# A hybrid decoder step on one core: the token row of the expert products in SBUF or in PSUM

## The chip, the cores and the metric

The kernel runs on one core of one Trainium2 chip. The metric is the time of one execution on the device in microseconds, the median of several runs. The engines of the core are TensorE (PE in the profile; its weight loads are PEld), VectorE (DVE), ScalarE (ACT), GpSimd (POOL) and SyncE (SP). They share 16 DMA engines.

## What is computed

One layer of a decoder trunk, for 512 prompt tokens and 8 sample tokens, all in float32, D_MODEL = 1024. The first part (normalisation, an S5 and a Mamba-2 branch, an output projection) is not touched here. The second part is a retrieval of experts: every token asks 8 heads, every head finds 16 out of 16384 experts by two top-16 lists and a top-16 of their 256 sums, and every expert is one row of `expert_down` and one row of `expert_up`:

```
qv = (xb @ w_query).reshape(128, 8, 2, 128)
s = einsum('thsd,hskd->thsk', qv, keys)
sv, si = top_k(s, 16)                       # two halves of the key
fv, fi = top_k(sums of all pairs, 16)       # 16 experts of 16384
g = softmax(fv)
u = expert_down[eidx]                       # (token, head, 16, 1024)
act = gelu(einsum('thkd,td->thk', u, xb)) * g
v = expert_up[eidx]
out = einsum('thk,thkd->td', act, v)
```

For 520 tokens these are 520 x 128 rows of 4 KB from each of the two tables, 545 MB in all.

## The kernel before

The program runs in stages, one after the other. The last, `stage_peer`, holds the retrieval. Tokens lie in 4 blocks of 128 (one token to a partition), the samples in a last short block in which 64 partitions hold 8 tokens x 8 heads.

A **unit** is one head of one block: 32 units of tokens. A **step** g is half a unit, 8 of its 16 experts (`GATE = 8`); there are 64 steps of tokens and two of samples (`NSTEP` = 66, steps 64 and 65). The engines each have their own order of work, written out by hand, and meet in semaphores:

- GpSimd issues for every step 8 **down gathers** (`gather_down`, L1659): each is one indirect DMA that brings one expert's row of 1024 floats to each of the 128 tokens, 512 KB, into one buffer of a ring. Then it issues 8 **up gathers** (`gather_up`, L1675) of the step that lies `LAG = 4` steps back. The down gathers of an even step wait for the unit's top-k (`s_top`), and every second gather waits until the buffers it fills were read (`s_uused`, counted in products). Up gathers wait until TensorE has used the rows of the group before (`s_vused`).
- VectorE runs, for every step, 8 **products** (`products`, L1903): one instruction multiplies a gathered buffer by the token row and sums it up to one number per token; the product is written back over the buffer. The token row is `hb`, 128 x 1024, the block's normalised input, copied from `h2` once per block (L1943 and L1947). The sample steps take `x64`, which lies in SBUF, in its place. Between the products of an even and an odd step stands the top-k of the next unit (`topk`, L1859 to L1894). In units 0 to 6 VectorE also stores scores from PSUM. In the third unit of blocks 1 to 3 it closes the block before (L1921, L1923, L1934, L1938), in unit 8 it takes in the sample rows and in unit 9 the scales of the last normalisation.
- ScalarE makes gelu and softmax, and spreads the weights into the matrix Z.
- TensorE projects the queries and scores them in units 0 to 6, and sums the up rows with their weights (`add`, L1797 for tokens, L1805 for samples).

**Buffers.** SBUF is one tensor, `arena`, laid out by hand. Sixteen buffers of 128 x 1024 floats (`rows16`) lie where earlier stages had their data: the first 8 are those of the up rows, the other 8 belong to the ring of the down rows. Two more, `more`, lie behind the query's memory, and two, `late`, in the memory of the query weights, free only after unit 7. The ring is therefore `first_U` = 8 + 2 = 10 buffers in steps 0 to 15 (gathers 0 to 127) and `all_U` = 12 from step 16 (gather 128) on. What a gather waits for follows from the list of what was last in its buffer (`U_free`):

```
first_U, all_U = rows16[VR:] + more, rows16[VR:] + more + late
for i in range(GATE * NSTEP):
    ring = first_U if i < 2 * PH * GATE else all_U
    s = i % len(first_U) if i < 2 * PH * GATE else (i - 2 * PH * GATE) % len(all_U)
    U_free.append(used.get(s))
...
if j % 2 == 0 and U_free[i + 1] is not None:
    pool.wait_ge(s_uused, U_free[i + 1] + 1)
```

With rings of 10 and 12 an even gather i waits until i - 8 and i - 10 products are done; gather 128 is the first of the larger ring, which begins again at buffer 0: it waits until product 121 is done.

`hb` lies in PSUM before the change, banks 6 and 7.

Of the kernel before, what the change touches and what calls it, by code (L numbers as in the profile page):

```python
# [28 lines left out]
D = 1024  # L29
# [1497 lines left out]
def stage_peer(nc, mem, sem, ps, A, O, mod_d, integers):  # L1527
# [8 lines left out]
    def take(*shape, rows=P):  # L1536
        nonlocal M
        M += int(np.prod(shape))
        return mem(M - int(np.prod(shape)), *shape, rows=rows)
# [6 lines left out]
    late = [take(D) for _ in range(2)]  # L1546
    assert M <= Map.PEER
    M = Map.PEER
    more = [take(D) for _ in range(2)]
    Z = take(4, 8, 32)  # L1550
    sel64 = take(PH, NS, rows=NS)
    r64 = take(NS)
# [14 lines left out]
    sdiag = take(2 * GATE, NS)  # L1567
    stat, rstd = take(1), take(1)
    assert M <= Map.W, M
    hb = ps[:, 6:8, :].rearrange("p a n -> p (a n)")  # L1570
    idx = [integers["expert0"], integers["expert1"]]
    idxT = [integers["rows0"], integers["rows1"]]
    kix, fix, fiju, iotai = (integers[n] for n in ("keys", "pairs", "halves", "counting"))
# [426 lines left out]
def program(nc, A, O):  # L2000
    with nc.cleanup_on_exit(), ExitStack() as ctx:
        mem = Arena(ctx.enter_context(nc.sbuf_tensor("arena", [P, Map.W], F32)))
        ps = ctx.enter_context(nc.psum_tensor("ps", [P, 8, 512], F32))
        mod_d = nc.dram_tensor("mod_scratch", (NC_ROWS, NMOD * D), F32, kind="Internal").ap()
        bc_d = nc.dram_tensor("bc_scratch", (NS, D), F32, kind="Internal").ap()

        integers = {name: ctx.enter_context(nc.sbuf_tensor(name, [P, n], dtype))[:, :] for name, n, dtype in
                    (("expert0", TOPK, U32), ("expert1", TOPK, U32), ("keys", 2 * TOPK, U32), ("pairs", TOPK, U32),
                     ("halves", 2 * TOPK, U32), ("counting", TOPK, I32), ("rows0", 2 * TOPK, U32), ("rows1", 2 * TOPK, U32))}


        s_s5, s_ssd = nc.alloc_semaphore("first_s5"), nc.alloc_semaphore("first_ssd")

        for stage, more in ((constants, ()), (stage_condition, (ps, A, mod_d, s_s5)),
                            (stage_s5, (ps, A, O, s_s5, s_ssd)), (stage_ssd, (ps, A, O, bc_d, s_ssd)), (stage_query, (ps, A, mod_d)),
                            (stage_peer, (ps, A, O, mod_d, integers))):
            with nc.cleanup_on_exit():  # L2017
                stage(nc, mem, nc.alloc_semaphore, *more)
# [29 lines left out]
```

## Time and profile before

| | us |
|---|---|
| median of 3 runs (lowest, highest) | 2483.84 (2475.89, 2489.05) |
| the profiled execution, its own time | 2482.62 |
| its span (first to last instruction) | 2480.7 |
| VectorE busy | 1510.9 (61%) |
| GpSimd busy | 1090.3 (44%) |
| TensorE matmuls busy | 1365.7 (55%) |
| moved by GpSimd's DMA queue | 545.33 MB |

A busy time is a sum over the whole span, in which the expert stage is only the last 1500 us; what an engine is worth there has to be read from slices, groups and the timeline. A gather of 128 rows counts as busy on GpSimd while its descriptors are made, not while its data moves. A product is written CUSTOM_DVE_ANT_0 in the profile, and its tiles say where its inputs are: `arena` is SBUF, `ps` is PSUM.

### The profile page before, as it was taken

To read this page: it belongs to the slowest core of one execution; us is meant where nothing else is said; L and a number is where in the kernel's file an instruction comes from. 1 tells how busy PE (TensorE), PEld (TensorE's weight loads), DVE (VectorE), ACT (ScalarE), POOL (GpSimd) and SP (SyncE) were. 2 spreads that over 40 slices of the span, in tenths; PEclk is the share of its full clock that TensorE was granted. 3 is DMA by queue.
4 is the path that set the end of the run, shared out by engine and by line. 5 is a ranking of instruction groups with operands and counts; after the bars stand their busy time and mean duration, and the time that the engine had idled before them with its cause. 6 is when DMAs were issued, how large, how long until landed. Compare 5 with 4: busy or idle time off the path is not lost.

```text
span 2480.7 us, 19709 instructions
## 1 busy us (share of the span) xinstructions
PE 1365.7 (55%) x6380; PEld 764.8 (31%) x6380; DVE 1510.9 (61%) x3235; ACT 279.0 (11%) x575; POOL 1090.3 (44%) x1154
## 2 busy tenths in 40 slices
PE   4697997999644998556652222233233233233265
PEld 0276674878633845443320000000000000000010
DVE  0454998165688123777667776767776767676411
ACT  1011000111112002111110110000110001010000
POOL 0122000010130000476767777777777777777632
PEclk7798998999766999787866666655656665665555
DMA  9821000221332050799999999999999999999854
GB/s 367 315 64 52 34 34 0 87 73 37 94 94 93 2 189 26 296 365 403 409 403 409 409 406 409 409 406 405 406 401 396 409 409 405 408 403 407 279 145 152
DMA packets 209033, 651.98 MB, mean 263 GB/s; under 512 B 26192, under 2 KB 52464, under 8 KB 204793
## 3 DMA queue, kind: packets, MB, share of 16 engines
q0 software_dynamic: 150016, 545.33, 56.6%
q1 hardware_dynamic: 58092, 103.70, 11.8%
q10 hardware_dynamic: 824, 1.70, 0.2%
q8 instruction: 51, 0.84, 0.1%
q14 instruction: 50, 0.41, 0.0%
HBM read 643.24 MB, written 7.54 MB: 262 GB/s over the span
## 4 chain that ended last, share of the span: by engine, by line
DMA 21%; POOL 15%; issue 10%; PE 7%; DVE 7%; DVEq 0%; POOLq 0%; ACT 0%
DMA arena<-in_expert_up_dram,rows 16%; POOL arena L1675 8%; POOL arena L1659 7%; DMA arena<-in_expert_down_dram,expert 5%; PE ps L1797 4%; DVE arena L1903 2%; PE ps L1805 2%; DVE arena L1862 0%; DVE arena L1861 0%; PE ps L1344 0%; DVEq L1855 0%; DVE keys L1860 0%; DVE arena L1888 0%; DVE arena L1885 0%; DVE arena L1889 0%
## 5 line engine op out<-in xcount | busy, mean ns | idle before, releaser
L1797 PE MATMUL ps<-arena 128*32 128x512 f32 x2048 | 409.8, 942 | 831.1 <-DMA arena<-in_expert_up_dram,rows 831.1
L1903 DVE CUSTOM_DVE_ANT_0 arena<-arena,ps 128x1024 f32<-128x1024 f32 x512 | 617.1, 1219 | 317.0 <-DMA arena<-in_expert_down_dram,expert 301.7
L1675 POOL DMA_INDIRECT arena<-in_expert_up_dram,rows x512 | 490.6, 958 | 241.0 <-issue 136.4
L1659 POOL DMA_INDIRECT arena<-in_expert_down_dram,expert x528 | 501.3, 949 | 200.8 <-issue 155.8
L1797 PEld LDWEIGHTS ps<-arena 128*32 128x32 f32 x2048 | 81.9, 146 | 1120.1 <-issue 1120.0
L546 PE MATMUL ps<-arena 128*128 128x260 f32 x896 | 207.7, 391 | 14.8 <-ACT arena L477 7.8
L546 PEld LDWEIGHTS ps<-arena 128*128 128x128 f32 x896 | 173.0, 194 | 52.3 <-issue 16.2
L954 POOL MEMSET arena<- 128x528 f32 x2 | 1.1, 538 | 305.2 <-POOLq L2017 305.2
L1344 PE MATMUL ps<-arena 128*128 128x260 f32 x512 | 124.4, 404 | 4.9 <-POOL counting L1642 3.4
L1071 PE MATMUL ps<-arena 128*128 128x260 f32 x512 | 112.5, 383 | 0.0
L1344 PEld LDWEIGHTS ps<-arena 128*128 128x128 f32 x512 | 102.0, 202 | 28.9 <-issue 6.3
L1071 PEld LDWEIGHTS ps<-arena 128*128 128x128 f32 x512 | 97.2, 190 | 14.9
L1700 ACT ACTIVATE arena<-arena 128x8 f32<-128x8 f32 (+1 forms) x66 | 13.7, 208 | 748.1 <-DVE arena L1903 748.1
L970 POOL TENSOR_TENSOR arena<-arena 128x1024 f32<-128x1024 f32 x8 | 19.8, 2483 | 165.5 <-DVE arena L1230 126.7
L1459 PE MATMUL ps<-arena 128*128 128x512 f32 (+1 forms) x160 | 71.5, 610 | 8.2 <-DMA arena<-in_w_out_dram 8.2
L269 PE MATMUL ps<-arena 128*32 128x512 f32 x256 | 49.2, 910 | 44.8 <-DMA arena<-in_w_ada_dram 35.5
L1921 DVE TENSOR_TENSOR arena<-ps,arena 128x1024 f32<-128x1024 f32 (+1 forms) x5 | 6.1, 1220 | 91.6 <-PE ps L1805 70.7
L1805 PE MATMUL ps<-arena 64*8 64x512 f32 x64 | 54.8, 1053 | 5.7 <-DMA arena<-in_expert_up_dram,expert 5.7
L1167 PE MATMUL ps<-arena 128*128 128x260 f32 x256 | 57.5, 388 | 0.0
L456 POOL MEMSET arena<- 128x4096 f32 x1 | 3.5, 3512 | 113.4 <-POOLq L2017 113.4
L469 POOL COPY arena<-arena 64x16 f32<-64x16 f32 x64 | 31.6, 547 | 49.1 <-DVE arena L720 49.1
L1167 PEld LDWEIGHTS ps<-arena 128*128 128x128 f32 x256 | 49.5, 194 | 7.8
(347 smaller groups left out, 1878.4 us busy)
## 6 DMA issues: line engine op xcount, KB each, us to landing
arena<-in_w_ada_dram SPq DMA_DIRECT2D x12, 2048.0 KB
arena<-in_w_in_dram SPq DMA_DIRECT2D x11, 2048.0 KB, 8.4
arena<-in_expert_down_dram,expert POOLq DMA_INDIRECT x528, 12.6
arena<-in_w_ada_final_dram SPq DMA_DIRECT2D x4, 2048.0 KB
arena<-in_w_query_dram SPq DMA_DIRECT2D x8, 1024.0 KB, 16.4
arena<-in_expert_up_dram,rows POOLq DMA_INDIRECT x512, 12.1
out_dram<-arena SPq DMA_DIRECT2D x13, 512.0 KB, 2.9
arena<-in_x_prompt_dram SPq DMA_DIRECT2D x2, 2048.0 KB
```

The costliest lines, as they stand in the source:

```text
L269: last = nc.tensor.matmul(ps[strip(j, 32), i, :], cT[:, k, :], ring[q][:, k % 2, 512 * j:512 * j + 512], start=(k == 0), stop=(k == KD - 1))
L469: last = nc.gpsimd.tensor_copy(flat[:, 160 * q + 16 * g:160 * q + 16 * g + 16], bb[rows, j, 4 * ut + q, :])
L546: last = nc.tensor.matmul(ps[:, 5 + h, 0:HALF], ring[i % 2][:, k, m * P:(m + 1) * P], hT[:, k, h * HALF:(h + 1) * HALF], start=(k == 0), s ...
L1071: last = mm(ps[:, 2 * (n % 2) + h, 0:HALF], ring[i % 2][:, k, m * P:(m + 1) * P], hT[:, k, h * HALF:(h + 1) * HALF], start=(k == 0), stop= ...
L1167: last = mm(ps[:, 4 + 2 * (m % 2) + h, 0:HALF], brw[:, k, m * P:(m + 1) * P], cv[:, k, h * HALF:(h + 1) * HALF], start=(k == 0), stop=(k = ...
L1344: last = nc.tensor.matmul(ps[:, 2 + h, 0:HALF], self.ring[(t // 2) % 2][:, k, (t % 2) * P:(t % 2 + 1) * P], self.h2T[:, k, h * HALF:(h + 1 ...
L1459: last = mm(ps[0:n, 2 * (b % 2) + j, :], mg[:, k, b * P:b * P + n], wo[:, k, j * 512:(j + 1) * 512], start=(k == 0), stop=(k == KD - 1))
L1659: G.indirect_dma_start(U[i][0:rows, :], None, down, bass.IndirectOffsetOnAxis(ap=idx[u % 2][0:rows, k:k + 1], axis=0))\
L1675: G.indirect_dma_start(Vr[j], None, up, bass.IndirectOffsetOnAxis(ap=at, axis=0))\
L1797: last = mm(ps[32 * j:32 * j + 32, c, :], Z[:, j, m, :], Vr[4 * half + j][:, c * 512:(c + 1) * 512], start=(p % 4 == 0 and m == 0), stop=( ...
L1805: last = mm(ps[0:NS, 2 + c, :], sdiag[0:64, k, :], Vr[4 * half + j][0:64, c * 512:(c + 1) * 512], start=(k == 0), stop=(k == 2 * GATE - 1))
L1903: V.tensor_tensor_reduce(U[i][0:rows, :], U[i][0:rows, :], row, 1.0, 0.0, ALU.mult, ALU.add, dots[g % 2][0:rows, j:j + 1]).then_inc(s_uuse ...
```

## The change

`more` gets one buffer in the place of two, and the memory of the other becomes `hb`; the line that put `hb` into PSUM goes. Everything else follows from that: the rings have 9 and 11 buffers, an even gather waits until i - 7 and i - 9 products are done, gather 128 waits until product 127 is done (gather 127 was the last in buffer 1), the copies at L1943 and L1947 write to SBUF, and the 512 token products at L1903 read both inputs from SBUF. Banks 6 and 7 of PSUM stay empty in this stage.

```diff
--- before.py
+++ after.py
@@ -1546,7 +1546,8 @@
     late = [take(D) for _ in range(2)]
     assert M <= Map.PEER
     M = Map.PEER
-    more = [take(D) for _ in range(2)]
+    more = [take(D)]
+    hb = take(D)
     Z = take(4, 8, 32)
     sel64 = take(PH, NS, rows=NS)
     r64 = take(NS)
@@ -1567,7 +1568,6 @@
     sdiag = take(2 * GATE, NS)
     stat, rstd = take(1), take(1)
     assert M <= Map.W, M
-    hb = ps[:, 6:8, :].rearrange("p a n -> p (a n)")
     idx = [integers["expert0"], integers["expert1"]]
     idxT = [integers["rows0"], integers["rows1"]]
     kix, fix, fiju, iotai = (integers[n] for n in ("keys", "pairs", "halves", "counting"))
```

## Rows read from the trace of the kernel before

**Rows 1.** Page, part 2: GB/s in 40 slices of the span, 62 us each.
```profile
GB/s 367 315 64 52 34 34 0 87 73 37 94 94 93 2 189 26 296 365 403 409 403 409 409 406 409 409 406 405 406 401 396 409 409 405 408 403 407 279 145 152
```

**Rows 2.** Page, part 5: line, tiles xcount | busy, mean ns | idle.
```profile
L1903 DVE CUSTOM_DVE_ANT_0 arena<-arena,ps 128x1024 f32<-128x1024 f32 x512 | 617.1, 1219 | 317.0 <-DMA arena<-in_expert_down_dram,expert 301.7
L1675 POOL DMA_INDIRECT arena<-in_expert_up_dram,rows x512 | 490.6, 958 | 241.0 <-issue 136.4
L1659 POOL DMA_INDIRECT arena<-in_expert_down_dram,expert x528 | 501.3, 949 | 200.8 <-issue 155.8
```

**Rows 3.** Timeline, steps 16, 24, 25, 63: start, length (us), what.
```profile
1315.66 0.93 POOL L1659 DMA_INDIRECT arena<-in_expert_down_dram,expert  x1 [0.31 <-issue]
...
1316.90 0.94 POOL L1659 DMA_INDIRECT arena<-in_expert_down_dram,expert  x1 [0.30 <-issue]
...
1503.00 1.22 DVE L1903 CUSTOM_DVE_ANT_0 arena<-arena,ps 128x1024 f32<-128x1024 f32 x1
...
1504.28 1.22 DVE L1903 CUSTOM_DVE_ANT_0 arena<-arena,ps 128x1024 f32<-128x1024 f32 x1
...
1508.42 0.93 POOL L1659 DMA_INDIRECT arena<-in_expert_down_dram,expert  x1 [0.30 <-issue]
...
1515.85 1.21 DVE L1903 CUSTOM_DVE_ANT_0 arena<-arena,ps 128x1024 f32<-128x1024 f32 x1
...
2294.24 0.94 POOL L1659 DMA_INDIRECT arena<-in_expert_down_dram,expert  x1 [0.31 <-issue]
```

**Rows 4.** Waits of GpSimd, 1000 to 2300 us: total us, times, longest.
```profile
POOL arena L1675 <- PE ps L1797: 53.9, 46, 5.5
```

**Rows 5.** Groups by shape, VectorE, 900 to 2480 us: sample products.
```profile
L1903 DVE CUSTOM_DVE_ANT_0 arena<-arena 64x1024 f32<-64x1024 f32 x16 | 19.1, 1215 | 31.8 <-DMA arena<-in_expert_down_dram,expert 31.5
```

**Rows 6.** Timeline, GpSimd and VectorE, sample products (step 64).
```profile
2342.12 1.21 DVE L1903 CUSTOM_DVE_ANT_0 arena<-arena 64x1024 f32<-64x1024 f32 x1
...
2342.16 1.98 POOL L1675 DMA_INDIRECT arena<-in_expert_up_dram,rows  x1 [0.30 <-issue]
...
2343.26 1.21 DVE L1903 CUSTOM_DVE_ANT_0 arena<-arena 64x1024 f32<-64x1024 f32 x1
...
2344.41 1.21 DVE L1903 CUSTOM_DVE_ANT_0 arena<-arena 64x1024 f32<-64x1024 f32 x1
...
2344.45 1.99 POOL L1675 DMA_INDIRECT arena<-in_expert_up_dram,rows  x1 [0.30 <-issue]
...
2345.56 1.21 DVE L1903 CUSTOM_DVE_ANT_0 arena<-arena 64x1024 f32<-64x1024 f32 x1
...
2346.74 0.94 POOL L1675 DMA_INDIRECT arena<-in_expert_up_dram,rows  x1 [0.30 <-issue]
```

**Rows 7.** Timeline at the closing of the first block of tokens.
```profile
1442.95 1.28 DVE L1934 SCALAR_TENSOR_TENSOR arena<-arena 128x1024 f32<-128x1024 f32 x1
...
1443.43 1.61 POOL L1659 DMA_INDIRECT arena<-in_expert_down_dram,expert  x1 [0.30 <-issue]
```

**Rows 8.** Timeline, the first two of the eight products of step 21.
```profile
1433.82 1.21 DVE L1903 CUSTOM_DVE_ANT_0 arena<-arena,ps 128x1024 f32<-128x1024 f32 x1
...
1434.96 1.22 DVE L1903 CUSTOM_DVE_ANT_0 arena<-arena,ps 128x1024 f32<-128x1024 f32 x1
```

**Rows 9.** Timeline: gathers of steps 2, 4, 15; last product of 15.
```profile
1023.17 0.94 POOL L1659 DMA_INDIRECT arena<-in_expert_down_dram,expert  x1 [14.95 <-DVE expert L1894]
...
1031.88 0.94 POOL L1659 DMA_INDIRECT arena<-in_expert_down_dram,expert  x1 [0.30 <-issue]
...
1056.89 0.94 POOL L1659 DMA_INDIRECT arena<-in_expert_down_dram,expert  x1 [14.13 <-DVE expert L1894]
...
1295.46 0.94 POOL L1659 DMA_INDIRECT arena<-in_expert_down_dram,expert  x1 [0.30 <-issue]
...
1316.15 1.22 DVE L1903 CUSTOM_DVE_ANT_0 arena<-arena,ps 128x1024 f32<-128x1024 f32 x1
```

**Rows 10.** Page, part 6: DMA issues, count, median us to landing.
```profile
arena<-in_expert_down_dram,expert POOLq DMA_INDIRECT x528, 12.6
```

## What the change does to the time, forecast before it was run

> **What bounds the kernel now.** I read the slices of the span first [rows 1]: from about 1080 us to 2310 us the 16 DMA engines are full and move some 405 to 409 GB/s. That is the expert stage, and the change touches nothing else. The groups by cost [rows 2] name its parts: 512 products on VectorE (L1903) with 317 us of idle time before them, so VectorE is not the limit; and 528 down and 512 up gathers on GpSimd, which issues them one by one. Next I looked for the second limit behind the DMA engines. In the timeline one gather follows the other after 1.24 us (1315.66 to 1316.90), so a step of 16 gathers needs 16 x 1.24 = 19.8 us of GpSimd; the products come every 1.28 us (1503.00 to 1504.28), one transfer of the full DMA engines, so a step needs 16 x 1.28 = 20.5 us of DMA; and from step 16 (1315.66) to step 63 (2294.24) a step really takes 978.6 / 47 = 20.82 us [rows 3]. GpSimd thus has about 1.0 us of slack in a step, 5%. It shows in the waits as 53.9 us in which GpSimd waited for the up products on PE (L1797), 46 times [rows 4]. The kernel is bound by DMA with GpSimd right behind.
>
> **The change part by part.** *The product itself.* Its second input moves from PSUM to SBUF. The same operation with both inputs in SBUF is in the trace: the 16 sample products, 1215 ns against 1219 ns [rows 2, 5]. Between -4 and +4 ns on 512 products is at most 2 us of an engine that idles 317 us: nothing.
>
> *What two SBUF inputs do to a gather.* This term decides. The sample products run back to back at 2342.12, 2343.26, 2344.41 and 2345.56, each 1.21 us. The gather issued at 2342.16 takes 1.98 us instead of 0.94, the next (2344.45) 1.99, and the one at 2346.74, which starts as the last product ends, again 0.94 [rows 6]. At the end of a block of tokens, a gather issued at 1443.43 beside a two-input operation that runs from 1442.95 to 1444.23 takes 1.61 [rows 7]. All three fit one reading: about 0.13 us after its start a gather reads its indices from SBUF; if a VectorE operation with two SBUF inputs runs then, it waits until that one ends, and has 0.81 us left: 2343.33 + 0.81 = 2344.14, as in the row; 1444.23 + 0.81 = 1445.04, as in the row. Beside token products, whose row stands in PSUM, nothing of the kind happens: over all 512 up gathers the mean is 958 ns [rows 2]. After the change all 512 token products do what the sample products do.
>
> The Trainium skill (SBUF — State Buffer, section Who interferes with whom) says the same in general: a VectorE instruction with two SBUF inputs contends with a GpSimd instruction that reads SBUF, and whichever issues first holds the shared pair for its whole length. The rows agree with the first half and not with the second: the product at 2343.26 starts and ends in 1.21 us while the gather of 2342.16 still runs. By the rule's second half VectorE would also lose time; that is the fourth rival.
>
> *What that costs in a step of the long stretch.* The eight products fill about 10.2 us of 20.8. A gather that meets them at a random point waits on average half a product, 0.61 us. After that the two engines march together: released at the end of a product, GpSimd tries again 0.81 + 0.30 + 0.13 = 1.24 us later, and if products come every 1.28 us [rows 3] the next one ends 0.04 us after that. So the other seven cost 0.04 each, 0.3 us. If the down gathers, themselves delayed, come in with a gap, the meeting at a random point happens a second time; I take one and a half meetings, 0.9 us. Where a product follows after less than 1.24 us (data already there: 1.14, as at 1433.82 [rows 8]), the gather just misses the end and waits for the one after: period 2.28, 1.04 us lost per gather, as in the sample rows. I take a third of a miss per step, 0.4 us. Need of GpSimd: 19.8 + 0.9 + 0.3 + 0.4 = 21.4, against 20.8 now: +0.6 us. Lower bound of the step's extra: 0, if all of it fits into the slack. Upper: all products at 1.14, four gathers at 2.28 in 9.1 us, +4.2 and the meeting 0.6, less the slack of 1.0: +3.8. I take the value near the rows of 1.28, since a longer step makes products wait for arrivals, which spaces them at 1.28 again. 43 ordinary steps x 0.6 = +26 us; +0 to +163.
>
> *Five steps with a late VectorE* (three closings of a block, and the two that take in the sample rows and the final scales) run their products at 1.14 [rows 8]: 4.2 + 0.6 - 1.0 = +3.8 each, +19 us; between 0 and +24.
>
> *Steps 4 to 15*, with the query projection beside them, take (1295.46 - 1056.89) / 11 = 21.7 us [rows 9], slack 1.9. Odd steps have more products at 1.14 behind the score stores: a pair loses about 1 + 4.2 = 5.2 against a slack of 3.8; six pairs, +8 us; 0 to +25.
>
> *Steps 0 to 3* are bound by the chain product, top-k, gather. The eight gathers from 1023.17 to 1031.88 run beside products at 1.14; at 2.28 they take 16 us instead of 8.7, some 7 us more, of which about 5 reach the last product and the top-k that frees the gather at 1056.89 [rows 9]. Two such pairs: +10 us; 0 to +15. Nothing later gives this back, since the DMA engines are full from there on.
>
> *The rings.* With 10 buffers the first gather of a step waits for all products of the step before the last, with 9 for one product more; with 12 and 11 the gather at place 4 of a step needs two and three products of the step before. The gather at 1508.42 is one at place 4; all eight of those products had ended by 1504.28 + 1.22 = 1505.50 [rows 3]. So one buffer costs nothing there, and would not even if a step ran 2.9 us late. At the change of rings (gather 128) there is one place: it now needs product 127, which starts at 1316.15, while the gather was issued at 1315.66 [rows 3, 9]: 1316.15 + 1.22 - 1315.66, 1.7 us, once. Taken: +2 us; 0 to +6 with the first steps.
>
> *Four copies of the token row* pass over 1024 elements as a product does, 1219 ns [rows 2]. No row here stands for one within SBUF; each can save at most those 1.2 us, or cost half as much again. The first lies in the wait for the first gather, the others in VectorE's idle time: 0 (-4 to +2).
>
> Sum: 26 + 19 + 8 + 10 + 2 = +65 us. The profiled execution took 2482.62 us (span 2480.7), 1.2 below the median 2483.84, so the sum gives 2548 by the one and 2549 by the other. I say **2548 us**, +2.6%.
>
> **The rivals.** (1) *Absorbed.* The waits of the long stretch fit the slack of 1.0 us (0.6 + 0.3 = 0.9), VectorE's late steps too; what is left is steps 0 to 3 and the ring: +0 to +12, 2490 us. For it: the waits for PE [rows 4]. Against: it leaves 0.1 us, so any miss breaks it. (2) *The slow cadence wins.* Products stay bunched at 1.14, gathers at 2.28: 43 x 3.8 + 24 + 25 + 15 = +227, 2710 us. Counting from the other side gives the same size: half of 1040 gathers meet a product and wait 0.6 each, 310 us, less 60 steps' slack of 1.0, +250. Against: the ordinary steps run at 1.28. (3) *Not slower.* A step takes 20.82 where 16 transfers need 20.5; if this 0.3 is the price of about ten gathers queued at the DMA engines (12.6 us from issue to landing, 1.28 each [rows 3, 10]), a GpSimd that issues a little later gives it back in 47 steps, -15 us, provided its need stays below 20.5, that is, waits of at most 0.7 a step, and the first steps lose nothing: 2468 us. Against: one and a half meetings alone are 0.9. (4) *Held both ways.* A gather also stops products: each of the two waits for the other, 1.22 + 0.94 = 2.16 us a product, two steps of VectorE 16 x 2.16 + 10.3 of top-k (1505.50 to 1515.85 [rows 3]) = 44.9 against 41.6 now; 3.3 / 2 x 60 = +99, 2582 us. Against: the product at 2343.26. (5) *Only the rings matter* and the token products don't disturb gathers (the row moves but nothing waits): +2 to +15 with 12 ring-bound steps of one transfer each, 2490 us. Against it: [rows 6]. The same section of the Trainium skill infers that a two-tensor operation leaves the making of descriptors alone, since it takes only the read side of the pair; by that this rival would win, but the 1.98 us of a gather beside such an operation speak against it.
>
> **How the numbers follow.** My forecast (waits with the 1.28 cadence, with its own spread 2515 to 2600) 0.58; between it and the slow cadence, ending at 2600 to 2710, 0.19; held both ways 0.05; absorbed 0.11; rings alone 0.03; not slower 0.04. The range 2500 to 2665 leaves out the absorbed cases, the gain and the top of the slow cadence, about 2 in 10. A measurement here tells about 0.5% (12 us) from no change: slower 0.85, within 0.12, faster 0.03; half of the absorbed case and most of the "not slower" case fall within.
>
> **What would show it.** Right: down and up gathers beside token products with durations from 0.95 to 2.0 us, mean duration of L1675 and L1659 up from 0.95 to about 1.02 to 1.1 (each 0.1 us is 104 us of GpSimd, of which the slack takes some 55); the ordinary step about 21.4 us; GpSimd's wait for PE L1797 almost gone; DMA slices between 390 and 400 GB/s; gather to landing shorter than 12.6 us, since fewer are queued; products still 1.22 us. Wrong: gathers at 0.94 beside products (then 5), products longer than 1.22 (then 4), most spacings 1.14 with gathers at 1.98 (then 2), waits of gathers for L1903 growing (the rings).

## The result, and the profile after

The changed kernel took 2498.13 us (median of 5 runs, 2494.81 to 2504.29), the kernel before 2480.41 on the same chip: ratio 1.0072, interval 1.0045 to 1.0099, 18 us slower. A second set gave 1.0077 (1.0061 to 1.0093). The direction was forecast; 65 us were forecast and 18 came, below the range.

The page of the changed kernel (span, part 1, part 2, groups, landing), to be read against [rows 1, 2, 10]:

```profile
span 2496.2 us, 19710 instructions
...
GB/s 367 312 77 38 34 34 0 87 73 36 93 93 94 31 158 66 254 359 403 409 406 386 387 392 409 409 408 409 399 409 409 408 407 391 395 409 407 314 126 151
...
L1903 DVE CUSTOM_DVE_ANT_0 arena<-arena 128x1024 f32<-128x1024 f32 (+1 forms) x528 | 640.6, 1225 | 367.4 <-DMA arena<-in_expert_down_dram,expert 351.3
L1675 POOL DMA_INDIRECT arena<-in_expert_up_dram,rows x512 | 533.5, 1042 | 196.9 <-issue 149.0
L1659 POOL DMA_INDIRECT arena<-in_expert_down_dram,expert x528 | 527.8, 1000 | 197.2 <-issue 156.5
...
arena<-in_expert_down_dram,expert POOLq DMA_INDIRECT x528, 8.9
```

The gathers are longer on GpSimd: 958 to 1042 ns for the up rows, 949 to 1000 for the down rows, 512 x 0.084 + 528 x 0.051 = 70 us more. The product is hardly longer: 1226 ns with its shapes kept apart, 1219 before.

```profile
L1903 DVE CUSTOM_DVE_ANT_0 arena<-arena 128x1024 f32<-128x1024 f32 x512 | 621.5, 1226 | 330.8 <-DMA arena<-in_expert_down_dram,expert 314.9 <-issue 0.7
```

The 70 us show up as 15 in the span because GpSimd had time to give. Its waits for the up products on TensorE, 53.9 us from 1000 to 2300 us before [rows 4], are nearly gone: 9.0 us after (below). And the gathers queue for 8.9 us instead of 12.6.

```profile
POOL arena L1675 <- PE ps L1797: 9.0, 17, 2.7
```

Where the time went is read from the first down gather of each step. Lateness against the kernel before, in us, from the timelines (step 0 began 1.8 earlier in the changed kernel; "row" and "rings" are experiments told below):

```
first gather of step   0     5     16    24    36    52    63    end of span
changed kernel        -1.8  +8.8 +10.0 +16.8 +14.6 +16.2 +17.0  +15.5
changed, second set   +3.3 +13.5 +14.8 +20.9 +22.7 +24.5 +24.8  +23.4
row alone (row_only_2) +0.8  +9.8 +11.8 +19.4 +16.2 +18.6 +19.4  +16.6
rings alone (_2)      -0.4  +0.5  +3.3  +0.5  -0.4  +0.5  +0.6   +4.4
```

Two stretches carry it: steps 0 to 4 (+10.6) and steps 16 to 23 (+6.8). Steps 5 to 15 add 1.2, the 39 steps from 24 to 62 nothing here and in row_only_2, 3.9 in the second set. The first stretch, in the timeline of the changed kernel:

```profile
1024.01 1.22 DVE L1903 CUSTOM_DVE_ANT_0 arena<-arena 128x1024 f32<-128x1024 f32 x1
1024.05 1.99 POOL L1659 DMA_INDIRECT arena<-in_expert_down_dram,expert  x1 [0.30 <-issue]
...
1025.15 1.22 DVE L1903 CUSTOM_DVE_ANT_0 arena<-arena 128x1024 f32<-128x1024 f32 x1
...
1026.30 1.22 DVE L1903 CUSTOM_DVE_ANT_0 arena<-arena 128x1024 f32<-128x1024 f32 x1
1026.35 1.99 POOL L1659 DMA_INDIRECT arena<-in_expert_down_dram,expert  x1 [0.30 <-issue]
```

Four of the eight down gathers of step 2 take 1.99 us and start 2.29 or 2.30 apart, two products of 1.14 or 1.15, as the sample products showed [rows 6]; the first takes 1.14 us, the sixth 1.77, and the last two, behind the products, 0.94. The last of step 2 goes out at 1036.54, 13.9 us after the first, where it was 8.7 [rows 9]. Those gathers feed the next products and these the top-k, so the lateness stays.

An ordinary step, here 24:

```profile
1507.01 0.94 POOL L1659 DMA_INDIRECT arena<-in_expert_down_dram,expert  x1 [0.30 <-issue]
1507.49 1.23 DVE L1903 CUSTOM_DVE_ANT_0 arena<-arena 128x1024 f32<-128x1024 f32 x1 [9.85 <-DMA arena<-in_expert_down_dram,expert]
1508.26 1.27 POOL L1659 DMA_INDIRECT arena<-in_expert_down_dram,expert  x1 [0.30 <-issue]
...
1508.77 1.23 DVE L1903 CUSTOM_DVE_ANT_0 arena<-arena 128x1024 f32<-128x1024 f32 x1
...
1509.84 0.97 POOL L1675 DMA_INDIRECT arena<-in_expert_up_dram,rows  x1 [0.30 <-issue]
```

The products begin at 1507.49. By the reading of the prediction the gather of 1508.26 tries to read SBUF at 1508.39, waits for the end of the product at 1508.72 and takes 1.27 us; the next tries 0.03 before the end of the next product (1509.97 against 1510.00) and takes 0.97. One meeting of 0.33 us and seven of 0.03: this is the march at 1.28 us that was forecast. (The rows show the point at which a gather is held, 0.13 us after its start; that it is the reading of its indices is not shown.) The steps themselves, by their first gathers (24, 25 and 26), are 20.49 and 20.46 us long:

```profile
1499.55 0.94 POOL L1659 DMA_INDIRECT arena<-in_expert_down_dram,expert  x1 [0.31 <-issue]
...
1520.04 0.94 POOL L1659 DMA_INDIRECT arena<-in_expert_down_dram,expert  x1 [0.30 <-issue]
...
1540.50 0.94 POOL L1659 DMA_INDIRECT arena<-in_expert_down_dram,expert  x1 [0.31 <-issue]
```

A late step, 21, whose products are bunched as in [rows 8], shows the other cadence again:

```profile
1446.58 1.22 DVE L1903 CUSTOM_DVE_ANT_0 arena<-arena 128x1024 f32<-128x1024 f32 x1
1446.62 1.99 POOL L1675 DMA_INDIRECT arena<-in_expert_up_dram,rows  x1 [0.30 <-issue]
...
1448.91 1.99 POOL L1675 DMA_INDIRECT arena<-in_expert_up_dram,rows  x1 [0.30 <-issue]
...
1451.20 1.99 POOL L1675 DMA_INDIRECT arena<-in_expert_up_dram,rows  x1 [0.30 <-issue]
```

### The profile page after: what moved, and what is told of

The parts are those of the page before. It is cut to its first block, busy times and chain, and to the rows that moved or that the text cites. A ratio compares the mean times of both kernels' runs of the same rounds, so it can differ in the third digit from the quotient of the medians.

```text
span 2496.2 us, 19710 instructions
## 1 busy us (share of the span) xinstructions
PE 1361.8 (55%) x6380; PEld 766.9 (31%) x6380; DVE 1513.2 (61%) x3235; ACT 279.1 (11%) x575; POOL 1157.0 (46%) x1154
## 4 chain that ended last, share of the span: by engine, by line
POOL 24%; issue 17%; DMA 12%; PE 6%; DVE 2%; DVEq 0%; POOLq 0%; ACT 0%
POOL arena L1675 12%; POOL arena L1659 11%; DMA arena<-in_expert_up_dram,rows 11%; PE ps L1797 3%; PE ps L1805 2%; DMA arena<-in_expert_down_dram,expert 1%; DVE arena L1903 0%; DMA arena<-in_expert_up_dram,expert 0%; PE ps L1358 0%; DVE arena L1862 0%; DVE arena L1861 0%; DVE arena L1370 0%; DVEq L1855 0%; POOL arena L1679 0%; DVE keys L1860 0%
## 5 line engine op out<-in xcount | busy, mean ns | idle before, releaser
L1903 DVE CUSTOM_DVE_ANT_0 arena<-arena 128x1024 f32<-128x1024 f32 (+1 forms) x528 | 640.6, 1225 | 367.4 <-DMA arena<-in_expert_down_dram,expert 351.3
L1675 POOL DMA_INDIRECT arena<-in_expert_up_dram,rows x512 | 533.5, 1042 | 196.9 <-issue 149.0
L1659 POOL DMA_INDIRECT arena<-in_expert_down_dram,expert x528 | 527.8, 1000 | 197.2 <-issue 156.5
L546 PEld LDWEIGHTS ps<-arena 128*128 128x128 f32 x896 | 171.3, 193 | 51.2 <-issue 16.3
L1344 PEld LDWEIGHTS ps<-arena 128*128 128x128 f32 x512 | 103.2, 205 | 28.8 <-issue 5.8
L1071 PEld LDWEIGHTS ps<-arena 128*128 128x128 f32 x512 | 97.3, 190 | 14.8
L1921 DVE TENSOR_TENSOR arena<-ps,arena 128x1024 f32<-128x1024 f32 (+1 forms) x5 | 6.1, 1220 | 89.6 <-PE ps L1805 68.1
```

What stands on the lines that cost most here:

```text
L546: last = nc.tensor.matmul(ps[:, 5 + h, 0:HALF], ring[i % 2][:, k, m * P:(m + 1) * P], hT[:, k, h * HALF:(h + 1) * HALF], start=(k == 0), s ...
L1071: last = mm(ps[:, 2 * (n % 2) + h, 0:HALF], ring[i % 2][:, k, m * P:(m + 1) * P], hT[:, k, h * HALF:(h + 1) * HALF], start=(k == 0), stop= ...
L1344: last = nc.tensor.matmul(ps[:, 2 + h, 0:HALF], self.ring[(t // 2) % 2][:, k, (t % 2) * P:(t % 2 + 1) * P], self.h2T[:, k, h * HALF:(h + 1 ...
L1659: G.indirect_dma_start(U[i][0:rows, :], None, down, bass.IndirectOffsetOnAxis(ap=idx[u % 2][0:rows, k:k + 1], axis=0))\
L1675: G.indirect_dma_start(Vr[j], None, up, bass.IndirectOffsetOnAxis(ap=at, axis=0))\
L1903: V.tensor_tensor_reduce(U[i][0:rows, :], U[i][0:rows, :], row, 1.0, 0.0, ALU.mult, ALU.add, dots[g % 2][0:rows, j:j + 1]).then_inc(s_uuse ...
```

## Experiments: rings and row apart

Each kernel is the one before the change with the edit shown; ratios are against the kernel before on the same chip, in interleaved runs. The sets ran on five chips of two kinds. Two take 2480 and 2484 us for the kernel before (on one ran before_2, after_2, row_only_2 and rings_only_2, on the other row_first_2, row_24on, ps_pad and sb_pad), three take 2636 to 2651. So only ratios within a set compare; "the faster chip" and "the slower chip" stand below for a chip of either kind.

**rings_only, rings_only_2**

```diff
-    more = [take(D) for _ in range(2)]
+    more = [take(D)]
+    take(D)
```

> The row stays in PSUM, the rings have 9 and 11 buffers, and the freed buffer is left unused. Theory A (the change costs by the gathers that wait for two-input products, and the rings cost next to nothing): +0 to +3 us against the kernel before, gathers at 0.94 to 0.96 us on average. Theory B (the smaller rings cost, above all in the first steps, where a gather of a down row now needs one more product, and at gather 128): +10 to +18 us.

> Row in PSUM, rings of 9 and 11. In the first set 1.004 times the kernel before (1.001 to 1.007). Theory A: +0 to +3 us on a chip that runs at 20.8 us a step, since there the gathers have 9 us in hand. Theory B: +10 us here too.

Measured 1.0040 (1.0009 to 1.0071) on the slower chip, +11 us, which is in the range of theory B, and 1.0025 (1.0013 to 1.0038), +6 us, on the faster, more than the 3 us of theory A and less than the 10 of theory B. On the faster chip the steps of its trace lie within 2 us of the kernel before, except at the change of rings, where gather 128 waits (3.3 us late at step 16, 3.1 at step 17, 0.5 at step 24). Gathers are untouched:

```profile
L1676 POOL DMA_INDIRECT arena<-in_expert_up_dram,rows x512 | 488.9, 955 | 243.7 <-issue 138.2
```

What it has more lies behind step 63, where the last steps end 4 us later; but a second trace of the unchanged kernel ends 5 us later in the same place, so the trace doesn't settle it. That rings cost in the first steps (theory B) is refuted for the faster chip: +0.9 us at step 5. Where the 11 us of the slower chip lie isn't known.

**row_only, row_only_2**

```diff
-                row = hb if g < 2 * NU else x64[0:64, :]
+                b = g // (2 * PH)
+                row = x64[0:64, :] if g >= 2 * NU else h2[:, b * D:(b + 1) * D] if True else hb
```

> The token products read the row directly from h2 in SBUF, the rings keep 10 and 12 buffers (the copies into PSUM are still made, nobody reads them). Theory A: +13 to +17 us against the kernel before, like the whole change; mean of the up gathers near 1.04 us. Theory B: +0 to +3 us.

> Token products read the row from h2 in SBUF, rings of 10 and 12. Theory A: within 5 us of after_2. Theory B: less than after_2 by what rings_only_2 costs, 10 us or more.

1.0092 (1.0075 to 1.0109), +21 us at 2501.54, against 1.0077 for the whole change in the same set (after_2): the row alone is the whole cost, and taking a buffer away on top costs nothing that can be measured, though alone it cost 6 us. By the medians the two costs would add up to 28 us (theory B of after_2), and 20 were measured. Mean of the up gathers:

```profile
L1675 POOL DMA_INDIRECT arena<-in_expert_up_dram,rows x512 | 531.3, 1038 | 197.2 <-issue 151.2
```

On the slower chip the row alone cost 35 us, 1.0146 (1.0101 to 1.0191), more than the 13 to 17 us expected; its interval just touches that of the faster chip.

**before_2, after_2** repeat the two kernels.

> The kernel before once more, for its trace beside the others of this set. The chip of the first set took 2636 us for it in place of 2480, and showed VectorE and ScalarE stopping for 1 to 5 us inside the top-k with nothing waited for. If this set lands on such a chip, steps 16 to 63 take 23 to 24 us each; if not, 20.8.

> The changed kernel once more. Theory A (gathers wait for two-input products, rings nearly free): +15 to +20 us over the kernel before on a chip that runs at 20.8 us a step; on one that stops for instructions +35 to +45, as with the row alone. Theory B (both halves of the change cost on their own and add up): the sum of rings_only_2 and row_only_2.

before_2 (one run, 2485.72) has the first trace's steps to 0.3 us from step 10 on, after its start: the table above can be read to about 1 us within the steps. after_2 took 2500.26.

## Experiments: which steps pay

The same edit with another condition in the place of `True`: `g < 2 * PH` (steps 0 to 15), `g >= 2 * PH` (16 to 63), `g >= 24`, and `2 * PH <= g < 24`.

> As before the change, but steps 0 to 15 read the row from SBUF; rings of 10 and 12. The trace of the changed kernel was 8.8 us late when step 5 began and 10.1 us at step 16. Theory A: +8 to +12 us, in steps 2 and 4, whose gathers run beside bunched products. If the later steps cannot give anything back, it stays to the end.

> The row from SBUF in steps 0 to 15 alone, rings of 10 and 12, like row_first of the first set. On a chip at 2480 us for the kernel before: +8 to +11 us, all of it there when step 5 begins, and not given back. If the rest of the kernel can absorb a late start, less than 5.

> As before the change, but steps 16 to 63 read the row from SBUF; rings of 10 and 12. Theory A with the forecast's random meetings: +0.6 us in each of 43 steps, +26 us and more. Theory A with waits that settle into the slack of GpSimd: ordinary steps at 20.5 to 20.8 us, no cost, and only the bunched steps 17, 19 and 21 cost, +4 to +8 us in all. Theory B: 0.

> The row from SBUF in steps 24 to 63 alone. Random meetings (the forecast): 37 ordinary steps at +0.6 and two late ones at +3.8, +25 to +30 us. Waits that settle into GpSimd's slack: 0 to +4 us, with ordinary steps whose one meeting costs about 0.3 us each time.

> The row from SBUF in steps 16 to 23 alone. In the traces with the row in SBUF throughout, steps 16 to 24 took 7 us longer than before, steps 24 to 63 one or two; the row from step 24 on cost 2.7 us and in steps 0 to 15 9.9, of the 23 of the row alone. If the parts add up and the late VectorE of steps 17, 19 and 21 is the cause: +6 to +11 us. If those 7 us came from the first steps' lateness: +0 to +3.

> The row from SBUF in steps 16 to 23 alone, once more, since the last set fell on a chip that takes 2651 us for the kernel before. At 2480 us for it: +6 to +11 if steps 16 to 24 are late by the row there, +0 to +3 if by the lateness of the first steps.

```
row in SBUF in steps     faster chip                slower chip
0 to 15                  1.0040 (1.0024 to 1.0056)  1.0045 (1.0014 to 1.0076)
16 to 63                 -                          1.0067 (1.0034 to 1.0100)
16 to 23                 -                          1.0012 (0.9978 to 1.0046), 1.0010 (0.9979 to 1.0042)
24 to 63                 1.0011 (0.9997 to 1.0025)  -
```

On the faster chip the first 16 steps cost 10 us, all there when step 5 begins (+9.5 by the timeline; 2 us of it are given back by step 23, which wasn't expected). The last 40 steps cost 2.7 us, by the interval at most 6; in the trace of row_24on the lateness grows by 4.9 us from step 24 to 63. Random meetings would have cost +25 to +30 there, and are refuted. The cost of steps 16 to 63 (row_late), +14 us by the medians, lies between what was expected of settling and of random waits, on a chip where a step takes 23.7 us. That the 7 us of steps 16 to 23 belong to the row there was meant to be shown by row_mid; both its sets fell on the slower chip, where the intervals, up to +12 us, hold both expectations. It stays open; what speaks for it is that the lateness grows there in all three traces with the row in SBUF, that row_first_2, just as late at step 5, doesn't grow there, and that row_24on doesn't either. Within the stretch it grows in the late steps: 17, 19 and 21 take 2.5, 3.4 and 2.3 us more than before.

## Experiments: taking GpSimd's slack away

**ps_pad, sb_pad**: four small memsets on GpSimd ahead of the up gathers of a step, without and with the edit of row_only.

```diff
                 kind, v = groups[n]
+                for _ in range(4):
+                    link(G.memset(mem(52868, 128), 0.0))
```

> The kernel before, with four small memsets of 128 x 128 on GpSimd ahead of the up gathers of every step, in an unused corner of SBUF: about 1.0 us more GpSimd time per step, nothing else. The token row stays in PSUM. GpSimd has 0.9 to 1.0 us of slack in a step: 0 to +10 us. The waits of the up gathers for TensorE vanish as they did in the changed kernel.

> The same memsets with the row in SBUF, rings of 10 and 12. If the meetings are random they cost 0.9 and more on top of the 1.0: +60 to +80 us over the kernel before. If they settle, the wait at the meeting shrinks first: need 19.8 + 0.3 + 1.0 = 21.1 and a meeting between 0 and 0.6, so +35 to +55 us. If the slack hid nothing and both costs were always free, no more than row_only, +23.

Timeline of ps_pad, and the up gathers of both pages (ps_pad, then sb_pad). With their waits for one another the memsets put 2.78 us between two gathers in the place of 1.24, so 1.54 us a step, more than the slack.

```profile
1609.98 0.94 POOL L1659 DMA_INDIRECT arena<-in_expert_down_dram,expert  x1 [0.30 <-issue]
1610.92 1.01 POOL L1667 MEMSET arena<- 128x128 f32 x4
1612.76 0.94 POOL L1677 DMA_INDIRECT arena<-in_expert_up_dram,rows  x1 [0.83 <-POOL arena L1667]
...
L1677 POOL DMA_INDIRECT arena<-in_expert_up_dram,rows x512 | 486.9, 951 | 219.1 <-issue 129.0
...
L1677 POOL DMA_INDIRECT arena<-in_expert_up_dram,rows x512 | 526.8, 1029 | 216.4 <-issue 144.9 <-POOL arena L1667 50.5 <-PE ps L1807 17.1
```

The memsets take the same time in both, 209 ns each. Measured: 2517.10 us, 1.0135 (1.0110 to 1.0161): +33 us; and 2594.27, 1.0454 (1.0428 to 1.0481): +113 us. Both are beyond what was expected: the memsets were half as long again as planned, and they used up the slack. With the slack used up the row in SBUF costs 77 us where it cost 21. Worked out from the timelines, means over the 42 ordinary steps between 16 and 62 (without the late 17, 19, 21, 37, 53), and over the 37 of them that don't stand behind a late step:

```
                         42 steps: length, us   waits     37 steps: length, us   waits
before                             20.81        0.12                20.71        0.08
after                              20.67        0.75                20.69        0.77
ps_pad (row in PSUM)               21.72        0.13                21.69        0.14
sb_pad (row in SBUF)               22.66        1.07                22.71        1.16
```

Waits are the gather time over 0.94 us each, in us a step.

From ps_pad to sb_pad gathers wait 0.94 us more and the step is 0.94 longer: every microsecond of waiting costs one. From before to after they wait 0.63 more and the step isn't longer at all. That the slack hides it is shown. It is also used up: beyond the 0.30 us that lie between any two gathers GpSimd stands idle for 0.78 us in an ordinary step before, and 0.02 after.

On the slower chips it isn't hidden whole, though a step of 23.5 us leaves GpSimd over 3 us: over steps 16 to 62 gathers wait 2.1 us a step in row_only and 0.1 in rings_only, and the steps take 24.1 and 23.5 us. So the rule holds for the steady steps of the faster chips; why a part is paid on the others isn't shown.

A finding in the same traces: in the changed kernel the waits of the even steps are not random. The eighth down gather of the even steps, the one that meets the first product, and the distance from the first gather of a step to its first product:

```
even steps 24 to 34, after    1.27 1.27 1.30 1.29 1.79 1.27 us    7.9 7.9 8.0 7.9 8.5 7.9 us
even steps 36 to 42, after    (met elsewhere)                     9.2 9.3 9.2 9.1
even steps 44 to 50, after    (met elsewhere)                     10.5 10.4 10.4 10.4
even steps 54 to 62, after    1.38 1.27 1.29 1.20 1.27            8.0 7.9 7.9 7.9 7.9
even steps 24 to 34, before   0.94 in all                         12.6 12.2 12.8 13.1 13.0 12.0
```

The distance stands at 7.9, 9.2 or 10.4, a gather period of 1.24 apart. The odd steps are less regular: the gather that meets the first product takes 0.94 to 1.75 us there. I read it as a balance: while GpSimd is quicker than the DMA engines its queue grows, the products begin later, a gather meets them earlier in a product and waits longer, until GpSimd's step is the DMA engines' 20.48 us (16 x 1.28); 22 of the 42 ordinary steps are 20.40 to 20.49 us long. In sb_pad there is no slack to settle into, and the gather that meets the first product takes 1.04, 0.94, 1.27, 1.30, 1.56 and 1.03 us in steps 24 to 34.

One count in the traces speaks against the balance as the reason for small waits. Over the 42 ordinary steps the gather that meets the first product waits 0.34 us on average in the changed kernel, 0.31 in its second set, and 0.33 in sb_pad, where there is no slack. What grows in sb_pad are the later ones: 23 gathers behind the first meeting wait more than 0.5 us, against 5.

**ps_pad1, sb_pad1 and their repeats** (one memset instead of four, `range(1)`) were to test the balance.

> One memset of 128 x 128 per step on GpSimd, 0.4 us (four took 1.54 a step), row in PSUM. It fits into the slack: 0 to +4 us, ordinary steps still 20.8.

> The same 0.4 us a step with the row in SBUF, rings of 10 and 12. If the meeting of gathers and products settles so that GpSimd's step equals the DMA engines' 20.48, the memset is paid by the meeting: the gather that took 1.27 to 1.30 us in each even step now takes 0.95 to 1.1, and the whole costs +23 (the row alone) to +35 us. If meetings were random, the durations keep their spread around 1.3 and the memset adds its full 0.4 a step, +23 + 26 = +49 us.

> One memset of 0.4 us a step, row in PSUM: 0 to +4 us, ordinary steps 20.8.

> One memset of 0.4 us a step, row in SBUF, rings of 10 and 12. Meetings that settle: the meeting gather falls from 1.27 to 1.30 to 0.95 to 1.1 us, and the whole is +23 to +35 us. Random meetings: durations keep their spread, +49 us.

All four fell on the slower chip and don't test it: 0.9989 (0.9961 to 1.0017) and 1.0048 (1.0020 to 1.0077) in one set, 0.9920 (0.9889 to 0.9952) and 1.0036 (1.0002 to 1.0069) in the other. That the small memset makes the kernel faster there, by 0.8% in one set, isn't explained. There the step is 23.1 to 24.1 us and not held by the DMA engines (348 GB/s from 1400 to 2300 us in row_only, 406 in the kernel before on a faster chip): waits of VectorE in row_only there (total, times, longest), "issue" being time with nothing waited for, of which the faster chip has three pieces of 0.4 us in all:

```profile
DVE arena L1862 <- issue: 46.0, 19, 5.4
...
DVE arena L1883 <- issue: 20.3, 8, 3.8
...
DVE halves L1880 <- issue: 17.3, 11, 3.7
```

The balance is therefore argued, not shown.

## Why the prediction was wrong

*The mechanism was right.* A product with two inputs in SBUF makes a gather wait from 0.13 us after its start to the end of the product; 1.98 and 1.99 us beside bunched products, one meeting and then a march at 1.28 beside ordinary ones. The fourth rival fell: a product is not held up by a gather, 1226 ns against 1219. Rings alone: little, +6 us against the +2 forecast. Of the signs named beforehand the longer gathers, the vanished waits for TensorE and the shorter queue came; a step of 21.4 us and slices of 390 to 400 GB/s did not.

*Ordinary steps, forecast +0.6 each and +26 in all: the step that failed.* Measured over the 37 of them that don't stand behind a late step: 20.69 us against 20.71, -1 us in all. The waits were put at 0.9 + 0.3 + 0.4 = 1.6 us. They are 0.65 beside products: one meeting of 0.34 in the place of one and a half of 0.61, 0.18 for the march, and 0.13 for later gathers that wait longer, of which only 5 in 42 steps wait more than 0.5 us where a third of a miss a step had been taken. So the slack covers them, which is the rival "absorbed", given 0.11. The slack itself was put at 1.0 us from a mean that held late steps too; GpSimd's idle time was 0.78, so the row just fits. The case against the rival, that any miss breaks it, fell with the misses. With the slack gone the waits are 0.94 more, still short of 1.6. Why the meetings are smaller than random ones stays open.

*Late steps, forecast +3.8 each, +19:* their gathers do wait 2.7 to 4.1 us, against 0.5 to 1.4 before, and they take 22.6 to 24.0 us against 20.5 to 21.3. But the step behind each is shorter: over the five pairs 220.1 us against 212.2, +7.8, of which 5.7 lie in steps 17 to 22. I had let nothing be given back; that the seven to ten transfers then queued (8.9 and 12.6 us at 1.28 each) keep the DMA engines at work while GpSimd falls behind is my reading. It isn't whole: the three slices that hold steps 16 to 24 move 386 to 392 GB/s, where they moved 406 to 409.

*Steps 0 to 3, forecast +10:* from the first gather of step 0 to that of step 4 it is +5.2, to that of step 5 +10.6. The forecast had two bunched pairs there; but beside steps 0 and 1 the products come spaced by their data, about 2 us apart, and the pair grows by 1.2. The two steps that pay are 2 and 4. The size of a pair was right, the place one pair too early. *Steps 4 to 15, forecast +8:* +6.6, of which 5.4 is that step 4 and 1.2 the rest, where six pairs had been charged. Together +11.8 against +18, and the row alone in the first 16 steps cost 10. "Nothing later gives this back" was nearly so: 2 us were.

*Gather 128, forecast +2:* step 15 grew by 3.5 us, and step 16 starts later by no more than step 14 did. *Copies:* 686 ns in SBUF against 1220 into PSUM, without effect, as forecast.

The terms measured, 5.2 + 6.6 + 7.8 - 0.8, with the start 1.8 us earlier and 1.5 us less behind step 63, make the +15.5 of the span.

Of the rule of the Trainium skill (SBUF — State Buffer, Who interferes with whom): by the half in which the first to issue holds the pair for its whole length, products would have grown by nearly a gather; they grew by 7 ns. Its inference that a two-tensor operation leaves descriptor generation alone was held against it in the prediction, and these rows don't decide it: gathers are up to 1.05 us longer, but the 0.81 us that are left after the wait pass beside the next product without delay (2343.33 to 2344.14, beside the product of 2343.26 [rows 6]). What is held is a point 0.13 us after the start, not the rest.

## What to carry to other kernels

Keep one input of a VectorE operation in PSUM when GpSimd issues indirect gathers beside it, even where the place in PSUM buys nothing else; here it was worth 0.9%, a spare SBUF buffer 0.25%. Before a wait is charged to the time, find which engine sets the pace and how much slack the waiting one has in an ordinary step, not in the mean of all; and don't take a wait as random where two engines march in step. What is paid stands in stretches with bunched work (steps 2 and 4 here, and by the timelines 17, 19 and 21), and a cost that just fits the slack leaves none for the next one: four small memsets made the same row cost 77 us. Compare a step together with the one behind it: a step behind a late one is short in itself.

## Not expected of the hardware

Two engines with periods of 1.24 and 1.28 us march together at 1.28, but at 1.24 and 1.14 they drop to one gather for two products, 2.29 us. An ordinary step keeps its length, 20.71 and 20.69 us, whether its transfers queue for 12.6 us or for 8 to 9. And the same kernel took 2480 us on one chip and 2636 to 2651 on others, where in row_only VectorE stands for up to 5.4 us with nothing waited for, and there the row in SBUF cost 1.5%.
